# Conditioning sums of blocks 2 to 11: a 32x32 turn, a row sum and one pattern product for 8 one-column products

## What is computed

```python
c_act = jax.nn.silu(c)                                   # (1, 1024)
for layer in range(DEPTH):                               # 2 layers
    mod = c_act @ ada_w[layer] + ada_b[layer]            # (1, 1024) @ (1024, 6 * 1024)
    sh_m, sc_m, g_m, sh_f, sc_f, g_f = [t[:, None, :] for t in jnp.split(mod, 6, axis=-1)]
    hm = x * (1.0 + sc_m) + sh_m
    y = mixer(hm)
    x = layer_norm(RES_ALPHA * x + (1.0 + g_m) * y, ln_g[layer, 0], ln_b[layer, 0])
    hf = x * (1.0 + sc_f) + sh_f
    yf = swiglu(hf, ffn_w1[layer], ffn_w3[layer], ffn_w2[layer])
    x = layer_norm(RES_ALPHA * x + (1.0 + g_f) * yf, ln_g[layer, 1], ln_b[layer, 1])
```

## Time and profile before

| | |
|---|---|
| median of 3 runs | 1372.88 us (1363.7 to 1374.58) |
| span of the profiled execution | 1372.6 us |
| TensorE busy | 1332.3 us, 97%, 6566 matmul records |
| VectorE busy | 606.4 us, 44%, 826 instructions |
| ScalarE busy | 466.1 us, 34% |
| GpSimd busy | 507.1 us, 37% |
| mean granted TensorE clock | 0.988 of full speed |

### The profile page before, as it was taken

One profiled execution on the slowest core, in us unless ns is written; L12 is line 12 of the kernel. 1 busy time (PEld: TensorE's weight loads), 2 busy tenths in 40 slices (PEclk: granted clock), 3 DMA queues, 4 the chain that ended last, 5 costly groups with the idle time before them and its releaser, 6 DMA issues.

```text
span 1372.6 us, 17106 instructions
## 1 busy us (share of the span) xinstructions
PE 1332.3 (97%) x6566; PEld 1107.1 (81%) x6566; DVE 606.4 (44%) x826; ACT 466.1 (34%) x655; POOL 507.1 (37%) x209
## 2 busy tenths in 40 slices
PE   7999999999999999999899999999999999999996
PEld 6878877788888888888788777888888888887885
DVE  5489657767534343401746333268682110100005
ACT  3443253543222232112422344407342332232113
POOL 0343222324443444444344222212154444444444
PEclk9999999999999999999999899999999999999998
DMA  9962537523646465843335321112132322244322
GB/s 333 175 154 93 184 123 139 184 78 123 212 155 213 153 226 173 201 127 100 113 134 171 107 73 62 49 53 69 49 106 92 106 93 92 92 107 138 92 62 62
DMA packets 93539, 173.82 MB, mean 127 GB/s; under 512 B 15735, under 2 KB 61959, under 8 KB 93356
## 3 DMA queue, kind: packets, MB, share of 16 engines
q1 hardware_dynamic: 90344, 169.63, 40.7%
q10 hardware_dynamic: 3140, 3.43, 0.9%
HBM read 170.87 MB, written 4.52 MB: 128 GB/s over the span
## 4 chain that ended last, share of the span: by engine, by line
PE 82%; issue 9%; POOL 4%; DVE 2%; ACT 1%; DMA 1%; SPq 0%; POOLq 0%; DVEq 0%; ACTq 0%
PE ps L1128 15%; PE ps L1129 15%; PE ps L1130 15%; PE ps L1160 5%; PE ps L1161 5%; PE ps L1162 5%; POOL w_lo L697 3%; PE ps L1297 2%; PE ps L1299 2%; PE ps L1298 2%; PE ps L1657 1%; PE ps L1685 1%; PE ps L1311 1%; PE ps L1265 1%; PE ps L1266 1%
## 5 line engine op out<-in xcount | busy, mean ns | idle before, releaser
L697 POOL TENSOR_TENSOR w_lo<-raw,w_hi 128x1024 fp32r<-128x1024 f32 x192 | 475.0, 2479 | 823.7 <-ACT w_hi L751 823.5
L1128 PE MATMUL ps<-h_lo,w_hi 128*128 128x512 f32 (+2 forms) x1064 | 399.9, 376 | 7.5 <-POOL w_lo L697 5.0
L1129 PE MATMUL ps<-h_hi,w_hi 128*128 128x512 f32 (+2 forms) x1064 | 396.7, 373 | 0.0
L1130 PE MATMUL ps<-h_hi,w_lo 128*128 128x512 f32 (+2 forms) x1064 | 396.4, 373 | 0.0
L751 ACT ACTIVATE w_hi<-raw 128x1024 fp32r<-128x1024 f32 x198 | 207.9, 1057 | 495.0 <-DMA raw<-wstream 160.9
L1128 PEld LDWEIGHTS ps<-h_lo,w_hi 128*128 128x128 f32 (+1 forms) x1064 | 202.2, 190 | 48.2 <-issue 9.1
L1130 PEld LDWEIGHTS ps<-h_hi,w_lo 128*128 128x128 f32 (+1 forms) x1064 | 202.0, 190 | 35.3
L1129 PEld LDWEIGHTS ps<-h_hi,w_hi 128*128 128x128 f32 (+1 forms) x1064 | 202.2, 190 | 34.4
L2304 DVE TENSOR_TENSOR tmp<-tmp,ps 128x512 f32<-128x512 f32 x44 | 30.2, 687 | 261.1 <-PE ps L1130 261.1
L1160 PE MATMUL ps<-w_hi,hid_lo 128*128 128x512 f32 x336 | 131.0, 390 | 0.9 <-issue 0.9
L1162 PE MATMUL ps<-w_lo,hid_hi 128*128 128x512 f32 x336 | 130.7, 389 | 0.0
(11 more groups left out here) (293 smaller groups left out, 1639.9 us busy)
## 6 DMA issues: line engine op xcount, KB each, us to landing
raw<-wstream SPq DMA_DIRECT2D x205, 512.0 KB, 4.1
ada_raw<-astream SPq DMA_DIRECT2D x80, 512.0 KB, 4.3
ada_first<-astream SPq DMA_DIRECT2D x16, 256.0 KB, 6.7
ada_first<-astream SPq DMA_DIRECT2D x8, 512.0 KB, 10.4
ln_rows<-row_scratch SPq DMA_DIRECT2D x3, 1024.0 KB, 6.6
skew_scratch<-f_scratch ACTq DMA_DIRECT2D x1, 2304.0 KB
xa<-xT SPq DMA_DIRECT2D x4, 512.0 KB, 8.6
out<-xa SPq DMA_DIRECT2D x3, 512.0 KB, 3.5
```

What stands on the lines that cost most here:

```text
L697: nc.gpsimd.tensor_tensor(w_lo[:, slot, :], raw[:, slot % RAW, :], w_hi[:, slot, :].bitcast(F32), ALU.subtract).then_inc(sem("w_lo_ready"), 1)
L1128: pe.matmul(o, w_h, x_l, start=start, stop=False)
L1129: pe.matmul(o, w_h, x_h, start=False, stop=False)
L1130: return pe.matmul(o, w_l, x_h, start=False, stop=stop)
```

## The change

The sum over 128 partitions is done in three steps. VectorE turns each 32x32 square of `ada_acc` in place, so that the 32 partitions of a group come to lie along the row; a row sum over 32 leaves `ada_sum`, 128x32: for each group of 32 partitions and each column of the slot a partial sum. One product on TensorE with a 0/1 pattern, 1 where row and column agree modulo 32, adds the four groups and leaves each result on all four groups. `mod_block` then picks the right column for each group of 32 partitions, so it is four additions of 32x8 with a stride of 4. `C_SUM` takes the place of a constant that no instruction used. Turn and row sum (`ada_fold`) stand right behind the eighth slot, but for block 2 behind `v_blocks("vb")` and for block 3 ahead of `gla_gate((0, 1))`; in the loop they stand ahead of the second step. `ada_sum` adds 128 bytes per partition.

```diff
@@ -148,7 +148,7 @@
 
 
 
-C_IDENT, C_ONE, C_ZERO, C_KEEP, C_DROP, C_TRI, C_ONES = 0, 128, 129, 130, 258, 386, 514
+C_IDENT, C_ONE, C_ZERO, C_SUM, C_DROP, C_TRI, C_ONES = 0, 128, 129, 130, 258, 386, 514
 C_N = 642
 
 M_RESET, M_SEL, M_SAME, M_CAUSAL, M_WAUP = 0, 512, 1024, 1152, 1280
@@ -160,7 +160,7 @@
     r = np.arange(P)
     c[:, C_IDENT:C_IDENT + P] = np.eye(P)
     c[:, C_ONE] = 1.0
-    c[:, C_KEEP:C_KEEP + P] = r[:, None] < r[None, :]
+    c[:, C_SUM:C_SUM + P] = r[:, None] % 32 == r[None, :] % 32
     c[:, C_DROP:C_DROP + P] = r[:, None] >= r[None, :]
     c[:, C_TRI:C_TRI + P] = -(r[:, None] >= r[None, :]).astype(np.float32)
     c[:, C_ONES:C_ONES + P] = -1.0
@@ -242,6 +242,7 @@
     nmr = at("nmr", [P, TB])
     warm = at("warm", [P, 1])
     ones = at("ones", [P, 1])
+    ada_sum = at("ada_sum", [P, 32])
     arena = place[0]
     assert arena + 22528 * 4 <= 229344, arena
 
@@ -1306,10 +1307,9 @@
 
         def ada_cols(blk, bank=7):
 
-            pe.wait_ge(sem("ada_step"), KC * (blk + 1) if isinstance(blk, int) else KC * blk + KC)
-            for n in range(KC):
-                m = pe.matmul(ps[:, bank, n:n + 1], ada_acc[:, tile_of(n)], one_col, start=True, stop=True)
-            m.then_inc(sem("ada_cols"), 1)
+            pe.wait_ge(sem("ada_summed"), blk - 1)
+            pe.matmul(ps[:, bank, 0:32], cst[:, C_SUM:C_SUM + P], ada_sum[:], start=True, stop=True
+                      ).then_inc(sem("ada_cols"), 1)
 
         def turn_x(n):
 
@@ -1855,15 +1855,27 @@
         def mod_block(blk, bank=7):
 
             dve.wait_ge(sem("ada_cols"), blk + 1)
-            V.tensor_tensor(mod[:, blk, :], ps[:, bank, 0:KC], vcol(V_ADAB + blk * KC, KC), ALU.add).then_inc(sem("mod_ready"), 1)
-
-        def ada_block(blk, before=True, ks=range(KC)):
+            for q in range(4):
+                r = slice(32 * q, 32 * q + 32)
+                i = V.tensor_tensor(mod[r, blk, :], ps[r, bank, q:32:4], vec[r, V_ADAB + blk * KC:V_ADAB + (blk + 1) * KC], ALU.add)
+            i.then_inc(sem("mod_ready"), 1)
+
+        def ada_fold(total):
+
+            dve.wait_ge(sem("ada_step"), total)
+            link(V.transpose(ada_acc[:], ada_acc[:]))
+            V.tensor_reduce(ada_sum[:], ada_acc[:].rearrange("q (b i) -> q b i", i=32), mybir.AxisListType.X, ALU.add
+                            ).then_inc(sem("ada_summed"), 1)
+
+        def ada_block(blk, before=True, ks=range(KC), fold=True):
             if blk > 2 and before:
                 mod_block(blk - 1)
             for k in ks:
                 i = KC * blk + k
                 dve.wait_ge(sem(f"ada_landed{i % 2}"), 16 * ((i - 16) // 2 + 1))
                 ada_slot(i, ada_raw[:, i % 2, :], k == 0)
+                if k == KC - 1 and fold:
+                    ada_fold(KC * (blk + 1))
 
         def gate_col(i):
             dve.wait_ge(sem("mod_ready"), (3, 6, 9, 12)[i])
@@ -2042,8 +2054,9 @@
         ada_block(2, False, range(2, 4))
         states(1)
         conv(3)
-        ada_block(2, False, range(4, KC))
+        ada_block(2, False, range(4, KC), False)
         v_blocks("vb")
+        ada_fold(3 * KC)
 
         def gla_stats(tb):
 
@@ -2135,8 +2148,9 @@
             if h < 2:
                 ada_block(3, False, range(2 + 3 * h, 4 + 3 * h))
                 ml_stats(h)
-                ada_block(3, False, range(4 + 3 * h, 5 + 3 * h))
+                ada_block(3, False, range(4 + 3 * h, 5 + 3 * h), False)
             else:
+                ada_fold(4 * KC)
                 gla_gate((0, 1))
                 ml_stats(h)
         gla_gate((2, 3)).then_inc(sem("og_ready"), 1)
@@ -2326,10 +2340,19 @@
                         else:
                             V.tensor_scalar(ada_acc[:], ada_raw[:, 0, :], c_act[:, 0:1], None, ALU.mult
                                             ).then_inc(sem("ada_step"), 1)
+                    if u == 1:
+                        dve.wait_ge(sem("ada_step"), 8 * it + 48)
+                        V.transpose(ada_acc[:], ada_acc[:]).then_inc(sem("ada_turned"), 1)
+                        dve.wait_ge(sem("ada_turned"), it + 1)
+                        V.tensor_reduce(ada_sum[:], ada_acc[:].rearrange("q (b i) -> q b i", i=32), mybir.AxisListType.X, ALU.add
+                                        ).then_inc(sem("ada_summed"), 1)
                     step(2 * it + (u + 1))
                 dve.wait_ge(sem("ada_cols"), it + 6)
-                V.tensor_tensor(mod[:, bass.ds(it + 5, 1), :].rearrange("p o t -> p (o t)"), ps[:, 7, 0:KC],
-                                vec[:, bass.ds(KC * it + (V_ADAB + 5 * KC), KC)], ALU.add).then_inc(sem("mod_ready"), 1)
+                for q in range(4):
+                    r = slice(32 * q, 32 * q + 32)
+                    i = V.tensor_tensor(mod[r, bass.ds(it + 5, 1), :].rearrange("p o t -> p (o t)"), ps[r, 7, q:32:4],
+                                        vec[r, bass.ds(KC * it + (V_ADAB + 5 * KC), KC)], ALU.add)
+                i.then_inc(sem("mod_ready"), 1)
 
         ffn(0, norm(0, "out0"))
         gate_col(1)
```

## The result

| | before | after |
|---|---|---|
| median | 1373.45 us (8 runs, 1363.70 to 1377.21) | 1364.23 us (8 runs, 1363.63 to 1366.43) |
| profiled execution, span | 1372.6 us | 1362.5 us |
| ratio after / before, 95% interval | | 0.9942 [0.9923, 0.9962] |

The change gains 9.2 us, 0.6%, where 18.9 were forecast. The time lies just outside the upper end of the range.

The account below looks back on a forecast made before the run. TensorE, busy for 97% of the span, was taken to bound the kernel. Span 1372.6 less 13.7 us for the blocks and 5.1 for the clock gave 1353.8, so 1354 as median; range 1346 to 1364, likeliest case 1351 to 1358.

Parts of the forecast that it names:

- The working of each block: Each of ten conditioning sums on TensorE: eight products costing 1.79 us become one of 0.30, saving 1.49 us.
- the lower bound: Price of the new 32-column product on TensorE: 0.30 us with its seam, against 0.38 at the upper price.
- the careful end: VectorE's four additions in mod_block: none overlaps, 0.17 us each, taken as 0.5 us more per block.
- Block 3: Fold ahead of gla_gate((0, 1)): saves 0.45 us, not 1.49, with TensorE waiting 1 to 1.7 us before L1561's first matmul.
- The cover of the folds: VectorE's 2.5 us fold fits in its idle time, 5.85 us in a steady loop pass, so TensorE does not wait.
- a wait of 0.15: Block 11: fold delays the copy of kc1 to 729.85, TensorE wants it at 729.70; block saves 1.34 us.
- the faster panels would only wait longer for the copy of kc1: Reason to count no gain if the slow clock at 700 to 708, left in place, went.
- Saves 5 x 1.49: Loop blocks 5 to 9: the fold is hidden before the up product, so they save 7.45 us.
- The first and third stretch: Slow clock at 172 to 176 and 752 to 760 goes, gaining 5.1 us; second (700) and fourth (772) not counted.
- VectorE's fold shows: Rival, chance 0.14: a transpose of 3 to 6.7 us stalls blocks 3, 4 and 11; time 1363.
- The clock stretches stay or only move: Rival, chance 0.27: no gain from the clock, only the 13.7 us of the blocks; 1359.2, within 1358 to 1362.
- the likeliest case: The forecast itself, whole kernel: 1354 us, range 1351 to 1358, chance 0.45.

Follow-up runs that it names:

- e6: Changed kernel with ada_sum at the end of SBUF, its turns and row sums replaced by a memset of ada_sum: 1355.31 us, ratio to before 0.9898.
- e1: Changed kernel with only ada_sum moved behind the arena, so no earlier buffer shifts: 1358.26 us, ratio to before 0.9908.
- e5: Changed kernel with ada_sum at the end of SBUF, and block 11's slots 6 and 7 and fold behind the copy of kc1: 1351.61 us, ratio to before 0.9885.

## Why the prediction was wrong

**What held.** The working of each block: 1.49 forecast, 1.4 to 1.6 measured in all blocks but 3 and 9; the product at the lower bound and a little below. The fold, 2.5 us, from two neighbours' rows. Four additions in 0.68 us, 0.17 apart as at the careful end; by the rule of the Trainium skill, VectorE: DVE Perf Modes, section "Two Vector instructions with no wait between them", they are held one behind another, and the trace agrees. Block 3: 0.43 saved against 0.45, with the wait for og at 1.48 us in the forecast's 1 to 1.7, and by the way forecast: the two-source slot behind `mod_block(3)` stands behind a pass of GpSimd and takes 3.21 us, where such a slot alone takes 1.28 (VectorE and GpSimd after):

```profile
226.19 3.21 DVE L1852 SCALAR_TENSOR_TENSOR ada_acc<-ada_raw,c_act,ada_acc 128x1024 f32<-128x1024 f32 x1
```

```profile
225.67 2.65 POOL L698 TENSOR_TENSOR w_lo<-raw,w_hi 128x1024 fp32r<-128x1024 f32 x1 [5.27 <-ACT w_hi L752]
```

The fold has no part in that wait (1.5 in e6 too). The cover of the folds: e6 finds no cost in the loop or in block 3.

**The step that was missing.** The change part by part put a price on every instruction and none on the line `ada_sum = at("ada_sum", [P, 32])`. It stands in the diff ahead of `arena = place[0]`, and the text ahead of the prediction even says that it adds 128 bytes. It costs 6.1 us by the starts of the two projections and 6.0 by the medians of e1. No rival had it: nothing in the trace of before shows a price for a distance, and the first sign is a group of matmuls in after that is slower with nothing to explain it.

**The step that failed.** The prediction gave block 11 "a wait of 0.15". Its working was right in kind: fold ahead of the copy of kc1, TensorE due at 729.70. But it set both sides at their times of before, as if TensorE and the chain of slots would come earlier by the same amount. The actual sum: TensorE came to the first product of vc 13.87 us earlier, so it was due at 715.83. The chain of slots began at the `mod_block(10)` that moved only 11.4 us (704.01 to 692.60), and it took 25.4 us instead of 22.6, since transfers and the w_lo passes fed and slowed it. So the last slot ended at 717.96, fold and copy at 721.09, and 721.09 - 715.83 = 5.26. The prediction had the sentence for it: if the clock stretch at 700 went, "the faster panels would only wait longer for the copy of kc1". It went, 3.4 us, and that is what happened; it was treated as a reason to count nothing and not as a cost, with a slow clock behind the wait as well. Measured cost: 5.2 us for the wait and about 1.8 for the clock behind it.

**A smaller step.** "Saves 5 x 1.49" for blocks 5 to 9 looked at the handover of one steady pass. Behind block 9 the next work of TensorE is the down projection, and there the products had covered a gap: 0.64 us saved in place of 1.49.

**The clock.** 5.1 forecast, 6.3 in the two profiles. The first and third stretch went, as forecast, and the nine profiles against the five bear out both, the first without an exception. That the rest nearly cancels (the second gone, the fourth halved, two new ones) is luck. The 43 runs of the kernel before that stood beside the experiments have mean clocks from 0.985 to 0.996 and spans from 1361.7 to 1375.0 us, and in 15 of them, at 0.993 or more, the span is 1366.5 at most: those have most of this gain already. So most of the 9.2 us between the medians is the clock's. At clocks of 0.993 and 0.994 nine of these runs have a median span of 1364.9 us and the four of the changed kernel one of 1362.4: 2.5 us, near the 13.4 - 6.1 - 5.2 = 2.1 that the account leaves without the clock. Compared at the best clock seen, before spans 1361.7 us (0.996) and e5 1349.0 (0.996): 12.7 us, which is about the 13.7 forecast for the products' steps alone.

**The rivals.** "VectorE's fold shows" gives 1363 and is the nearest in time, but by a slow transpose and by stalls in blocks 3, 4 and 11; the transpose is fast and only block 11 stalls. It is not what happened. "The clock stretches stay or only move" is right for the fourth stretch and for the two new ones, and wrong for the other three.

With both steps mended, and two slots moved as well as the fold, e5 runs at 1351.61 us, in the likeliest case's own range.

## What to carry to other kernels

A line that allocates is part of the change: look at what it shifts, and above all whether it changes the distance between the two SBUF operands of the busiest matmul stage; here a distance of a multiple of 256 bytes kept the pace, and new small tiles belong behind the big ones. When a step takes time off an engine ahead of a handover, follow the other side's own chain to the same handover with its own releasers, since it need not move along; and a wait in front of a matmul stream can cost more than its length: here 5.3 us, and 1.8 of clock behind it. Work put "behind the last slot" should go behind what others wait for: moving two slots and a fold past one copy of 0.69 us brought 6.9 us, as much as four of the ten blocks' products.

## What the hardware showed that I had not expected

- The pace of f32r products with 128x128 stationary and 128x512 moving operands went with the distance between the two in SBUF: 0.2267 us at a distance that is a multiple of 256 bytes (three tried), 0.232 to 0.233 at 32, 64, 128 and -128 bytes from one, at a clock of 1.00 in all. Each distance but 0 and 128 rests on one profiled execution. Why isn't known. Whether other shapes show it was not tried, nor which operand has to be aligned to what beyond this pair.
- A 128x1024 fp32 turn in 32x32 squares costs 1.24 us, the same as a pass with two inputs and not the 0.75 of a plain pass.
- The granted clock fell during a wait of TensorE of 5.25 us (0.53 over its last 3.24 us) and was 0.72 on average over the 6.76 us behind it; without the wait (e5) it was 1.00 there.
- Eight fp32 products one column wide, 1.7 us of them, had a slow clock behind them at blocks 2 and 10 in nine profiles of nine; a single product 32 columns wide in their place had none in five of five.
